# The third layer's attention scores as three rounded products, and its first 21 slots three steps later

## What is computed

```
def odd_mixer(y, w_in, w_out, rel_table):
    proj = y @ w_in                                  # 1024 -> 3 * 1024
    q, k, v = jnp.split(proj, (C_DIM, 2 * C_DIM), axis=-1)   # 16 heads of 64
    ...
    bias = rel_table[:, idx]                         # by clipped distance
    o = chunk_band_attention(q, k, v, C_PREV_CHUNKS, bias, None)
    return o.reshape(B, S, C_DIM) @ w_out
```

## Time and profile before

| what | value |
|---|---|
| median of 3 runs | 2028.01 us (2027.89 to 2028.39) |
| the profiled execution | 2028.04 us |
| its span, first to last instruction | 2026.3 us |
| granted TensorE clock over the span | 1.000 |
| busy, share of the span | TensorE 99%, weight loads 87%, VectorE 72%, ScalarE 49%, GpSimd 12% |

### The profile page before, as it was taken

The page is one execution under the profiler, slowest core; times in us unless marked ns, Lnnn a source line. Parts: engine busy times, 40 slices in busy tenths (PEclk is TensorE's granted clock), DMA queues, the critical chain, the costliest instruction groups (busy, mean ns, idle before and its releaser), DMA issues.

```text
span 2026.3 us, 32634 instructions
## 1 busy us (share of the span) xinstructions
PE 2005.3 (99%) x12670; PEld 1757.3 (87%) x12670; DVE 1459.0 (72%) x2427; ACT 986.8 (49%) x1607; POOL 244.1 (12%) x266
## 2 busy tenths in 40 slices
PE   9999999999999999999999999999999999999998
PEld 7899988778899988988788899988877788999887
DVE  7888833786798863587778988933657779988733
ACT  5555622254445552453455555622557754555522
POOL 0000000500000000000002122000536520221001
PEclk9999999999999999999999999999999999999999
DMA  8322233312223223321321566333256624666232
GB/s 257 125 105 105 79 101 112 132 56 93 86 105 105 99 87 98 106 104 63 94 84 68 164 185 182 105 102 112 106 136 172 162 73 135 172 183 172 87 99 70
DMA packets 90141, 236.99 MB, mean 117 GB/s; under 512 B 47728, under 2 KB 51104, under 8 KB 73616
## 3 DMA queue, kind: packets, MB, share of 16 engines
q1 hardware_dynamic: 72896, 184.04, 27.6%
q0 software_dynamic: 14768, 37.49, 8.4%
q10 hardware_dynamic: 2336, 13.52, 1.9%
HBM read 211.86 MB, written 7.38 MB: 108 GB/s over the span
## 4 chain that ended last, share of the span: by engine, by line
PE 90%; DVE 6%; ACT 1%; issue 1%; DMA 0%; POOL 0%; SPq 0%; DVEq 0%
PE ps L1285 29%; PE ps L1286 28%; PE ps L1287 28%; DVE act L2556 1%; PE ps L512 1%; PE ps L525 1%; PE ps L736 1%; PE ps L718 1%; DVE w_lo L1784 1%; PE ps L703 1%; DVE w_lo L1794 1%; DVE w_sum_lo L2550 0%; DMA raw<-in_w_up 0%; PE ps L1272 0%; PE ps L1307 0%
## 5 line engine op out<-in xcount | busy, mean ns | idle before, releaser
L1794 DVE TENSOR_TENSOR w_lo<-raw,w_hi 128x2048 fp32r<-128x2048 f32 (+3 forms) x144 | 287.6, 1997 | 154.3 <-ACT w_hi L1766 146.3
L1285 PE MATMUL ps<-act,w_hi 128*128 128x512 f32 (+1 forms) x1026 | 376.3, 367 | 2.7 <-DVE w_lo L1794 1.6
L1286 PE MATMUL ps<-act,w_hi 128*128 128x512 f32 (+1 forms) x1026 | 372.0, 363 | 0.0
L1287 PE MATMUL ps<-act,w_lo 128*128 128x512 f32 (+1 forms) x1026 | 371.9, 362 | 0.0
L1285 PE MATMUL ps<-xq,w_hi 128*128 128x256 f32 x1024 | 290.6, 284 | 2.9 <-DVE up L2731 1.6
L1287 PE MATMUL ps<-xq,w_lo 128*128 128x256 f32 x1024 | 289.9, 283 | 0.0
L1286 PE MATMUL ps<-xq,w_hi 128*128 128x256 f32 x1024 | 289.9, 283 | 0.0
L1285 PEld LDWEIGHTS ps<-act,w_hi 128*128 128x128 f32 x1026 | 193.5, 189 | 40.4 <-issue 7.9
L1285 PE MATMUL ps<-xq,w_sum_hi 128*128 128x256 f32 x768 | 218.0, 284 | 1.7 <-ACT prod L2010 1.2
L1287 PEld LDWEIGHTS ps<-act,w_lo 128*128 128x128 f32 x1026 | 193.6, 189 | 30.0
L1286 PEld LDWEIGHTS ps<-act,w_hi 128*128 128x128 f32 x1026 | 193.7, 189 | 28.9
(11 more groups left out here) (301 smaller groups left out, 3977.3 us busy)
## 6 DMA issues: line engine op xcount, KB each, us to landing
raw<-in_w_up SPq DMA_DIRECT2D x87, 1024.0 KB, 4.8
raw<-in_w_down SPq DMA_DIRECT2D x29, 768.0 KB, 4.2
raw<-in_w_in SPq DMA_DIRECT2D x20, 1024.0 KB, 4.7
raw<-in_w_down SPq DMA_DIRECT2D x29, 640.0 KB, 3.8
raw<-in_w_out SPq DMA_DIRECT2D x8, 1024.0 KB, 4.8
w_sum<-in_w_up POOLq DMA_DIRECT2D x32, 256.0 KB, 4.4
raw<-raw POOLq DMA_DIRECT2D x32, 256.0 KB, 3.3
w_sum_odd<-in_w_up POOLq DMA_DIRECT2D x32, 256.0 KB, 4.3
```

The source lines that it names most:

```text
L1285: pe.matmul(own, hi, rhs_hi, start=start, stop=False, skip_group_check=more)
L1286: pe.matmul(own, hi, rhs_lo, start=False, stop=False, skip_group_check=more)
L1287: return pe.matmul(own, lo, rhs_hi, start=False, stop=stop, skip_group_check=more)
L1794: eng.tensor_tensor(w_lo[:, w], raw[:, w], w_hi[:, w].bitcast(F32), ALU.subtract).then_inc(lo_rounded, 1)
```

## The change

The scores are made of three rounded products instead of one plain product. For that each tile of the ring is split when it has been evicted: ScalarE writes its rounded part (`ring_high`), queries into chunk c of `mix_lo` and keys into chunk c of `mix_hi`, which are free until the pair's output is written there; VectorE then subtracts that part from the ring's chunk in place (`ring_rest`), which from then on holds the rest under the name `ring_lo`. For a tile that ends with step g the first is done at ScalarE's step g+1 and the second at VectorE's step g+2; for the last tile that is in out3's loops. A pair's first slot waits on TensorE for the key tile's rest. In a block the three parts come one after the other, each for both heads. The slots 0 to 20 come three steps later: 87, 92, 97, 103 and so on, up to 193, which is out3's first step. Slots 21 to 28 stay at 196 to 224.

```diff
@@ -133,7 +133,7 @@
 
     return q + 1 - sum(p <= q for p in PIECED)
 
-SLOTS = {84 + 16 * i // 3 if i < 21 else 196 + 4 * (i - 21): i for i in range(29)}
+SLOTS = {87 + 16 * i // 3 if i < 21 else 196 + 4 * (i - 21): i for i in range(29)}
 
 ATTENTIONS = [dict(back=1, ahead=1), dict(back=1, ahead=0)]
 
@@ -264,6 +264,8 @@
         s_t, reset, o_norm, o_sq = sq, gated, gate, prod
 
         ring = up_at("ring", 6 * T, 0)
+        ring_lo = at("ring_lo", [P, 6 * T], F32R, act_at)
+        ring_hi = lambda j: chunk((mix_lo, mix_hi)[j % 2], j // 2)
         v_tok = up_at("v_tok", 8 * T, 6)
         weigh = up_at("weigh", 4 * T, 14)
         turned = up_at("turned", 4 * T, 18)
@@ -341,6 +343,7 @@
         w_v_ps = sem("w_v_ps")
         w_v_done = sem("w_v_done")
         w_scores = sem("w_scores")
+        ring_hi_ready, ring_lo_ready = sem("ring_hi_ready"), sem("ring_lo_ready")
         w_max = sem("w_max")
         w_probs = sem("w_probs")
         w_normed = sem("w_normed")
@@ -501,16 +504,17 @@
                 if i == 0:
                     pe.wait_ge(w_v_done, KD)
                 if s == 0:
-                    pe.wait_ge(evacuated, IN3.g0 + 2 * c + 2)
+                    pe.wait_ge(ring_lo_ready, 2 * c + 2)
                 if i >= 2:
                     pe.wait_ge(w_max, rows_up_to(i - 1))
-                ks = (2 * c + 1) % 6 * T
+                q_hi, q_lo = ring_hi(2 * c), chunk(ring_lo, 2 * c % 6)
+                k_hi, k_lo = ring_hi(2 * c + 1), chunk(ring_lo, (2 * c + 1) % 6)
                 for n, at_, w in own:
-                    qs = 2 * c % 6 * T + n * P
-                    for hh in range(2):
-                        rows = slice(64 * hh, 64 * hh + 64)
-                        ins = pe.matmul(score_bank(i, hh)[:, at_:at_ + w], ring[rows, qs:qs + P], ring[rows, ks:ks + w],
-                                        start=True, stop=True)
+                    for part, (lhs, rhs) in enumerate(((q_hi, k_hi), (q_hi, k_lo), (q_lo, k_hi))):
+                        for hh in range(2):
+                            rows = slice(64 * hh, 64 * hh + 64)
+                            ins = pe.matmul(score_bank(i, hh)[:, at_:at_ + w], lhs[rows, n * P:(n + 1) * P], rhs[rows, 0:w],
+                                            start=part == 0, stop=part == 2)
                 ins.then_inc(w_scores, 1)
             u = i - 4
             if 0 <= u < STEPS:
@@ -543,6 +547,16 @@
             st, q = (IN3, IN3.q0 + pair) if pair < IN3.pairs else (OUT3, IN3.q0 + pair)
             eng.wait_ge(lo_rounded, q - 1)
             eng.dma_start(raw[:, q % 2 * PAIR:(q % 2 + 1) * PAIR], weights[st.name][q - st.q0]).then_inc(raw_landed[q % 2], 16)
+
+        def ring_high(eng, j):
+
+            eng.wait_ge(evacuated, IN3.g0 + j + 1)
+            eng.activation(ring_hi(j), chunk(ring, j % 6), ACT.Copy).then_inc(ring_hi_ready, 1)
+
+        def ring_rest(eng, j):
+
+            eng.wait_ge(ring_hi_ready, j + 1)
+            eng.tensor_tensor(chunk(ring_lo, j % 6), chunk(ring, j % 6), ring_hi(j).bitcast(F32), ALU.subtract).then_inc(ring_lo_ready, 1)
 
         def slot_act(eng, i):
 
@@ -2171,6 +2185,8 @@
                     for g in range(1, IN3_STEPS + 1):
                         if g in SLOTS:
                             slot_act(eng, SLOTS[g])
+                        if g > st.lead + KD and g % KD == 1:
+                            ring_high(eng, (g - st.lead) // KD - 1)
                         pair_load_act(eng, g)
                         round_piece(eng, pieces_at(IN3, OUT3, g))
                         if g == 28:
@@ -2193,6 +2209,8 @@
                     for g in range(1, KD * KD // 2 + 1):
                         if IN3_STEPS + g in SLOTS:
                             slot_act(eng, SLOTS[IN3_STEPS + g])
+                        if g == 1:
+                            ring_high(eng, IN3.groups - 1)
                         pair_load_act(eng, IN3_STEPS + g)
                         round_piece(eng, pieces_at(IN3, OUT3, IN3_STEPS + g))
                     break_out_act(st, BARRIERS[st.name])
@@ -2860,6 +2878,8 @@
 
                     for g in range(1, IN3_STEPS + 1):
                         j, to_end = (g - st.lead) // KD, -g % KD
+                        if g > st.lead + KD and g % KD == 2:
+                            ring_rest(eng, j - 1)
                         if g % (2 * KD) == 13:
                             rest_piece(eng, pieces_at(IN3, OUT3, g - 1))
                         if g in SLOTS and 0 < to_end < 4 and j < st.groups:
@@ -2883,6 +2903,8 @@
                 if st.name == "out3":
                     link(eng.memset(ssum[:, :], 0.0))
                     for g in range(1, KD * KD // 2 + 1):
+                        if g == 2:
+                            ring_rest(eng, IN3.groups - 1)
                         if IN3_STEPS + g in SLOTS:
                             slot_dve(eng, SLOTS[IN3_STEPS + g], link)
                         i, _, end = split_block(st, g)
```

## The result

The changed kernel takes 2032.01 us (median of 14 runs, 2031.43 to 2034.17); the kernel before, run beside it, 2028.13 us (14 runs, 2027.45 to 2028.57). The ratio is 1.0021, with a 95% interval of 1.0014 to 1.0028: 3.9 us slower, where the forecast was 0.7 us faster. The profiled execution took 2031.66 us, its span 2029.9 us, at a granted clock of 0.999; before it was 2028.04 and 2026.3 us.

What follows compares the result with a forecast made beforehand. TensorE, busy 2005.3 of 2026.3 us, was taken as the bound. Cheaper products (-1.7 us) and slot 21's wait (+1.0), with passes and move free, gave -0.7 us: 2027.3 us, range 2022.4 to 2034.2.

Steps and rivals of the forecast that it cites:

- The move by itself: Slots 0 to 20 three steps later: same order, TensorE has products to fill the steps; cost 0.
- slot 21's chain: From the last key tile's end through ScalarE's copies and exponentials to VectorE's subtraction: 5.6 us, against 4.4 us of cover.
- term 2: Sixteen rounding copies on ScalarE (9.9 us) and sixteen subtractions on VectorE (11.0 us) fit the spare time; cost nothing by amount.
- term 1: Score products on TensorE: 192 rounded ones replace 64 plain ones, -0.21 us a head pair, -1.7 us in all.
- term 3: TensorE waits for the subtracted keys ahead of a pair's first slot; only slot 21 loses time, +1.0 us.
- (a): Rival, slower: the two heads' rounded products on TensorE don't run side by side; 2041.7 us, chance 0.09.
- (b): Rival, slower: a weight load on TensorE doesn't run under a product of its own rows; 2034.1 us, chance 0.07.
- (c): Rival, slower: the wait for subtracted keys takes every pair, the chain being 2 us longer; 2035.3 us, chance 0.06.
- (d): Rival, faster: entering a slot on TensorE costs nothing any more, 24 slots win 4.8 us; 2022.5 us, chance 0.08.
- No slot waits for another engine: Reading of the earlier profile: score weight loads idle 8.5 us ahead of their 24 slots, released by "issue".

Runs made afterwards that it cites:

- last-tile run: Changed kernel with the last weight piece ahead of its slot, plus the last key tile rounded and subtracted ahead of slot 20: 2027.46 us, 0.9998 of the kernel before.

## Why the prediction was wrong

**Failed: "The move by itself", cost 0.** Its reason was "Nobody waits earlier than before, except slot 21". That looked at what the slots wait for and at what they issue, the queues among it, but not at the steps' own pieces, which stand behind a slot on ScalarE and VectorE and have due times that didn't move. The piece of step 92 + 16c had 2.4 to 3.9 us of margin. Of the 2.4 at step 97 the move took 2.8: it brought slot 1 three steps (2.04 us) nearer to the due step and put slot 2 behind that step, while the chain got 0.5 us shorter. "TensorE has products to fill the steps" overlooks that a slot's own products fill them too. It cost 4.5 us together with the passes, and 0.57 us alone. The prediction has one piece of this kind, the one of step 192 in slot 21's chain, and works out the margin of none.

**Failed with it: "Cost nothing by amount", term 2.** By amount it is right: at least 40 us are left on either engine (the busy time in the stretch grew by 7.4 us on VectorE and 7.9 on ScalarE, less than the 11.0 and 9.9 summed up), and with another order no cost of the same passes can be told. But that paragraph names their place ("behind a slot's own work") without asking what is queued behind them. The subtraction's wait of 1.48 us for ScalarE delays the next slot's maximum, and through it ScalarE.

**Held: term 1, the products.** -2.0 us measured for -1.7. Within a block parts follow in 0.11 to 0.12 us at 128 and 256 columns, 0.17 at 384 and 0.23 at 512, as listed; the first part of a block takes more, by 0.05 us in slot 0 and 0.11 us in slots 1 and 2. The slots changed by +0.04, -0.13 and -0.17 us for +0.06, -0.11 and -0.16. The loss on entering and leaving a slot stayed.

**Held: term 3, the wait.** Slot 21 waits 0.96 us for the subtraction, its slot is 1.07 us longer for +1.0, and none of the other pairs' first slots waits. The last-tile run shows the chain to be the one given. But that no other pair waits may be luck in part: with the weight stalls gone, slot 6 waits 0.50 us (the run with the piece ahead of the slot).

**Not foreseen: slot 27, 0.59 us.** It has no term in the sum. Its turned weights are late since the last transposing DMA was: issued at 1623.34, copied from 1629.45 on, after ScalarE had waited 4.02 us for it.

**The rivals.** (a), heads one after the other, falls: both heads' products stand in one row (x2), and at 384 columns the next part follows 0.17 us later, the time of one head's columns. (b), loads that don't run under a product of their own rows, falls too: at 384 columns the parts are 0.17 us apart, the time of their columns, while the stretch has as many weight loads as products (x991, x992). The second part's loads start while the first part's products, of the same rows (1493.30, 0.44 us long), still run:

```profile
1493.41 0.19 PEld L516 LDWEIGHTS ps<-ring_lo,act 64*128 64x128 f32 x2
```

There the Trainium skill ("TensorE: Matmul & The Clock Gate", section "Part 3: Packing small matmuls — row/col tiling") says that loads overlap only where the row group differs; these rows disagree. (c), the wait at every pair, came near in kind (a chain through ScalarE and VectorE, late at seven of the pairs), but the waiting instruction is a projection product, for weights. (d) falls with the gap that stayed. The measured time lies inside the range, which reaches up for (b)'s sake, but for a reason that was none of the rivals'.

**A reading that goes further than its rows.** "No slot waits for another engine" rests on the earlier trace rows, which are the score products' loads alone. The loads for the weighing did wait for turned weights before, 13 times and 8.6 us in all, while TensorE was busy with other products; that TensorE itself waited for nobody holds.

## What to carry to other kernels

When slots are moved against a stream of steps, list every item of the stream that stands behind a slot on each in-order engine, with the step at which it is due, and work out its margin from the profile before the move; a margin shows in no list of waits. Take off the steps of the move, and also the time of every slot that the move carries past the due step, for that work no longer covers the item. A pass that waits for another engine is costed by what it delays behind it, on its own engine and then on the engine it waits for, not by its length. If such an item turns out late, putting it ahead of the slot can give all of it back: 4.2 us of the median here, for a few lines.

## What the runs showed of the hardware

Rounded products with 128 columns are no cheaper than with 256: 0.11 us against 0.12 a part (slot 0 above), as long as a weight load takes to follow another.

The time of a transposing DMA varies with no change to it. From the issue of the last one to ScalarE's copy it takes 4.3 us before (1619.66 to 1624.01), 6.1 us after, 4.4 with the piece ahead of its slot, and about 6 with the tiles split ahead of the slots and without the subtraction. ScalarE stood waiting for it each time. The slowest of the 24 in a run takes from 5.3 us (before) to 9.2 (without the subtraction), the fastest 3.6 in every run. What delays them was not tried, so the cause stays open, and with it whether slot 27's 0.6 us belongs to the change.
